# A hybrid decoder layer on one core: sample rows of two norms kept as 128 rows, softmax and value pages at other blocks

## The chip, the cores and the metric

One core of a Trainium2 chip runs the whole layer in one launch. The metric is the device time of the launch in microseconds; the profile below is one execution of the same program.

## The reference, cut to what matters

The layer serves 256 new prompt tokens and 8 sample tokens (one per running sequence), 264 token columns in all, with 2048 channels (16 tiles of 128) and float32 throughout.

```
h  = rmsnorm(x, g1);  proj = h @ w_in               # q k v z xBC dt and two gates
attn = moba_attention(q, k, v)                      # samples: 8 sequences, 8 pages of 128 keys each
ssm  = mamba2(z, xBC, dt)                           # conv, chunked scan, group rmsnorm
m  = sigmoid(ga) * (attn @ w_attn_out) + sigmoid(gs) * (ssm @ w_ssm_out)
x1 = x  + rmsnorm(m @ w_out, g2)                    # second norm
f  = (silu(n @ w_gate) * (n @ w_up)) @ w_down,  n = rmsnorm(x1, g3)
y  = x1 + rmsnorm(f, g4)                            # last norm
rmsnorm(x, g) = x * rsqrt(mean(x*x over the 2048 channels) + 1e-6) * g
```

A sample selects 3 of its 4 past key blocks by score, adds its own key, and takes one softmax over them.

## The kernel before

**Blocks.** The matrix products run over 562 blocks on TensorE. A block is one tile of 128 output channels times eight tiles of input channels: 8 times three products (weights high x input high, high x low, low x high, lines 1733 to 1735), each moving the 264 token columns. Two adjacent output tiles are a pair and share two PSUM banks. Pairs follow a list: the input projection is blocks 0 to 209 (q, dt, k, v, then x, b, c, z and both gates mixed), `so` (w_ssm_out) starts at 210, `ao` (w_attn_out) at 242, `o` (w_out, 8 pairs of 4 blocks) at 258, `gate` and `up` at 290, and `dn` (w_down, 8 pairs of 12 blocks) at 466.

**How a block is fed.** ScalarE rounds the loaded weights to `w_hi` (four slots), VectorE computes `w_lo = raw - w_hi` (line 1197), TensorE waits for it. So ScalarE and VectorE can be at most about three blocks ahead of TensorE.

**Side work.** Every engine walks the same block numbers and issues at fixed numbers whatever else is due: on each engine the order is program order, with semaphores between engines. The numbers that the change touches are written out by hand:

- `K_AT[m] = 30 + int(K_PACE * m)` for the 64 key pages: GpSimd multiplies page m by the query at block K_AT[m] (line 740), VectorE sums it two blocks later (line 1391). With K_PACE 1.58 the last page is at block 129, with 1.61 at block 131.
- `SEL` starts the softmax of the samples. TensorE sums at SEL and SEL+3, VectorE selects at SEL+8 and SEL+9, TensorE turns the maxima at SEL+8 (this needs VectorE's SEL+9), VectorE normalises at SEL+20, and multiplies the own value row (`own_t`) at SEL+24.
- `VG[w]` starts the value pages of samples 2w and 2w+1: eight groups, two blocks apart, on TensorE (line 1985), with VectorE steps at VG+18 and VG+21. The first group waits for `own_t`.
- `UN[g]` are the eight groups of the norm in the state-space branch. VectorE takes the reciprocals at UN[g]+5 (line 1514). The input halves of `so` follow at blocks 211 to 214 (line 1522).

**The last two norms (pairs `o` and `dn`).** After each pair ScalarE leaves the squares of the pair in `sq` and the pair times the gain in `tmp` (128 channels x 264 tokens). `token_sums` on TensorE (from line 2016) turns `tmp` to token rows, per tile: two turns of 128 x 128 (line 1695) into `side[0]` and `side[1]`, and one of 128 x 8 into 8 rows of `side[2]` (line 1696: a plain float32 product with the identity as the moving operand, which appears as two instructions). After every fourth tile VectorE and ScalarE copy 512 columns of the rows out (`rows_of`). After the last pair TensorE sums the squares over channels into `side[3]` (line 2031), three chunks of tokens (128, 128 and 8 rows) times three parts. ScalarE takes the roots (`token_root`), VectorE the reciprocals (`token_rs`).

**Between `o` and `gate`.** `second_norm` on VectorE makes `x1tok = x + norm` in chunks (`x1_chunk`: two of 128 rows and one of 8 rows). TensorE turns it back, tile by tile (`x1_turn`: two turns of 128 x 128 and one of 8 x 128); ScalarE and VectorE make the halves `x_hi`, `x_lo` of the tile (`h_hi_of`, `h_lo_of`). Blocks 290 to 293 are `fresh_products`: per tile k, six products for both output tiles and then the turn of tile k+3. The first three turns lie ahead of the first product, with filler products between them (lines 2049 and 2053). ScalarE squares x1 beside it (`x1_squares`), and the next norm's factor is applied to the outputs of `gate` and `up`.

**The end.** After `dn`, VectorE updates `y` in twelve steps of 512 columns (three token chunks x four), each followed by its store.

Of the kernel before, what the change touches and what calls it, by code (L numbers as in the profile page):

```python
# [22 lines left out]
P = 128  # L23
# [28 lines left out]
K_PACE = 1.58  # L52
# [3 lines left out]
def bass_hybrid_decoder_layer(nc, a, o):  # L56
    ctx = ExitStack()
    with ctx:
# [152 lines left out]
        ftok_s = at("ftok_s", [NB, 2 * 512], fp32, 28 * K)  # L211
        y1s = at("y1s", [NB, D], fp32, E0)
        ftok_e = at("ftok_e", [NB, 2, 512], fp32, E0 + 8 * K)
# [100 lines left out]
        def evac_at(p):  # L314
# [13 lines left out]
        SEL = 130  # L328
        CT_AT = 214
        VG = [152 + 22 * w for w in range(4)]  # L330
        UN = [196, 198, 200, 201, 203, 205, 207, 208]
# [13 lines left out]
            "a_hi_done a_lo_done ao_sum ao_hi ao_lo tk_acc tk_sum tk_tr tk_cp0 tk_cp1 tk_sd m_x1 x1_back x1_out x1_in r2_sd "  # L345
# [9 lines left out]
         tk_tr, tk_cp0, tk_cp1, tk_sd, m_x1, x1_back, x1_out, x1_in, r2_sd, r2_diag, r2_mm, ff_tanh, ff_prod, ff_hi,  # L355
# [73 lines left out]
        y_order = [(0, 0), (0, 1), (1, 0), (1, 1), (0, 2), (1, 2), (2, 2), (2, 0), (2, 1), (3, 2), (3, 0), (3, 1)]  # L429

        def f_part(j, c):

            cols = slice(j * 512, (j + 1) * 512)
            if j == 3:
                return side[c][0:(P if c < 2 else NB), :]
            if c < 2:
                return ftok[:, c, cols]
            return ftok_s[:, cols] if j < 2 else ftok_e[:, 0, :]
# [12 lines left out]
        def _(sp):  # L451
# [157 lines left out]
            def x_again(b):  # L609

                if b == B_O + 8:
                    sp.wait_ge(ao_lo, KT)
                    for c in range(2):
                        sp.dma_start(x1tok[:, c, :], a["x_prompt"][0, c * P:(c + 1) * P, :]).then_inc(x1_back, 16)
                    sp.dma_start(x1tok[0:NB, 2, :], a["x_sample"][:, 0, :]).then_inc(x1_back, 16)
                if b == B_FF + 10:
                    sp.wait_ge(m_x1, 15)
                    for c in range(2):
                        sp.dma_start(x1_spill[c * P:(c + 1) * P, :], x1tok[:, c, :]).then_inc(x1_out, 16)
                    sp.dma_start(x1_spill[TP:T, :], x1tok[0:NB, 2, :]).then_inc(x1_out, 16)  # L620
                if b == B_DN + 8:
# [5 lines left out]
                    sp.dma_start(y1s[:, :], x1_spill[TP:T, :]).then_inc(x1_in, 16)  # L627
# [40 lines left out]
            sp.wait_ge(y_out, 16 * 12)  # L668
# [99 lines left out]
        def _(act):  # L768
# [28 lines left out]
            def h_hi_of(k, gain, m):  # L797

                act.wait_ge(x_tr, KT * m + k + 1)
                func(x_hi[:, k, :], h_bank[m][k % len(h_bank[m])][:, 0:T], scale=gains[:, gain, k:k + 1])\  # L800
# [235 lines left out]
            def rows_of(b, b0, step, base):  # L1036

                j, d = (b - b0) // step - 1, (b - b0) % step
                if 0 <= j < 3 and d == 7:
                    act.wait_ge(tk_tr, base + 4 * j + 4)  # L1040
                    if base:
                        act.wait_ge(mm_done, B_DN)
                        func(ftok[:, 1, j * 512:(j + 1) * 512], side[1][:, :])
                        func(f_part(j, 2), side[2][0:NB, :]).then_inc(tk_cp1, 1)
                    else:
                        cols = slice(j * 512, (j + 1) * 512)
                        func(mtok[:, 1, cols], side[1][:, :])
                        func(mtok[0:NB, 2, cols], side[2][0:NB, :]).then_inc(tk_cp1, 1)

            def token_root(n, summed):  # L1050

                act.wait_ge(tk_sum, summed)
                for c in range(3):
                    rows = P if c < 2 else NB
                    ins = func(nsd[0:rows, n, c:c + 1], side[3][0:rows, 2 * c:2 * c + 1], ACT.Sqrt,
                               bias=eps[0:rows, 0:1], scale=1.0 / D)
                ins.then_inc(tk_sd, 1)

            part = att_st[:, :, :].rearrange("p a b -> p (a b)")

            def x1_squares(j):

                act.wait_ge(m_x1, 3 * j + 6)
                cols = slice(j * 512, (j + 1) * 512)
                for c in range(3):
                    rows = P if c < 2 else NB
                    func(mtok[0:rows, c, cols], x1tok[0:rows, c, cols], ACT.Square,
                         accum_out=part[0:rows, 4 * c + j:4 * c + j + 1])

            def x1_root():  # L1070

                drained(func(mtok[0:1, 0, 0:1], x1tok[0:1, 0, 0:1]))
                for c in range(3):
                    rows = P if c < 2 else NB
                    ins = func(part[0:rows, 4 * c:4 * c + 4], part[0:rows, 4 * c:4 * c + 4],
                               accum_out=nsum[0:rows, 2, c:c + 1])
                drained(ins)
                for c in range(3):
                    rows = P if c < 2 else NB
                    ins = func(nsd[0:rows, 2, c:c + 1], nsum[0:rows, 2, c:c + 1], ACT.Sqrt, bias=eps[0:rows, 0:1],  # L1080
                               scale=1.0 / D)
# [7 lines left out]
            def evac(pr, i, p):  # L1089
# [82 lines left out]
        def _(dve):  # L1172
# [33 lines left out]
            def h_lo_of(k, gain, m):  # L1206

                dve.wait_ge(h_hi, KT * m + k + 1)
                stt(x_lo[:, k, :], h_bank[m][k % len(h_bank[m])][:, 0:T], gains[:, gain, k:k + 1],
                    x_hi[:, k, :].bitcast(fp32), ALU.mult, ALU.subtract).then_inc(h_lo, 1)  # L1210

            def token_rs(n):

                for c in range(3):
                    rows = P if c < 2 else NB
                    ins = v.reciprocal(nrs[0:rows, n, c:c + 1], nsd[0:rows, n, c:c + 1])
                drained(ins)
# [176 lines left out]
            def softmax(b):  # L1394
# [44 lines left out]
                if b == SEL + 24:  # L1439
# [101 lines left out]
            def x1_chunk(j, c0=0, c1=512):  # L1541
# [4 lines left out]
                for c in range(3):  # L1546
                    rows = P if c < 2 else NB
                    m = mtok[0:rows, c, cols] if j < 3 else side[c][0:rows, :]
                    x = x1tok[0:rows, c, cols]
# [562 lines left out]
```

## Time and profile before

| | us |
|---|---|
| median of 3 runs | 1809.43 |
| lowest and highest | 1805.69, 1809.56 |
| the profiled execution's own time | 1807.29 |
| its span in the trace | 1805.5 |
| TensorE busy | 1782.1 (99%) |
| VectorE busy | 1195.2 (66%) |
| ScalarE busy | 918.3 (51%) |
| GpSimd busy | 216.2 (12%) |

Matrix products overlap in the pipeline: a product of 264 columns is shown with 0.28 us, while the next starts 0.12 us later. So what an instruction costs TensorE is read from the starts of its neighbours, not from its duration. A row of the timeline can hold several instructions of one form in a row (x2, x8), with the time from the first start to the last end.

### The profile page before, as it was taken

To read this page: it belongs to the slowest core of one execution; us is meant where nothing else is said; L and a number is where in the kernel's file an instruction comes from. 1 tells how busy PE (TensorE), PEld (TensorE's weight loads), DVE (VectorE), ACT (ScalarE), POOL (GpSimd) and SP (SyncE) were. 2 spreads that over 40 slices of the span, in tenths; PEclk is the share of its full clock that TensorE was granted. 3 is DMA by queue.
4 is the path that set the end of the run, shared out by engine and by line. 5 is a ranking of instruction groups with operands and counts; after the bars stand their busy time and mean duration, and the time that the engine had idled before them with its cause. 6 is when DMAs were issued, how large, how long until landed. Compare 5 with 4: busy or idle time off the path is not lost.

```text
span 1805.5 us, 35392 instructions
## 1 busy us (share of the span) xinstructions
PE 1782.1 (99%) x14613; PEld 1719.1 (95%) x14613; DVE 1195.2 (66%) x1666; ACT 918.3 (51%) x1737; POOL 216.2 (12%) x127
## 2 busy tenths in 40 slices
PE   8999999999999999999999999999999999999997
PEld 8999999998988988889999899999999999999997
DVE  6478999999887557745744666666666666444443
ACT  5544556554766557533444655554545454444342
POOL 2145644564000000000000000000000000000000
PEclk9999999999999999999999999999999999999998
DMA  8589987897789999695564387767777775655552
GB/s 253 177 272 330 320 265 261 278 305 235 222 281 317 303 295 344 217 304 177 180 223 155 116 281 221 225 226 231 230 217 232 229 235 182 216 176 170 175 180 80
DMA packets 397810, 421.40 MB, mean 233 GB/s; under 512 B 13033, under 2 KB 375465, under 8 KB 396585
## 3 DMA queue, kind: packets, MB, share of 16 engines
q10 hardware_dynamic: 284336, 285.35, 49.5%
q1 hardware_dynamic: 112960, 133.11, 22.6%
q8 instruction: 115, 1.88, 0.4%
q0 software_dynamic: 352, 0.67, 0.2%
q14 instruction: 47, 0.38, 0.1%
HBM read 400.70 MB, written 18.66 MB: 232 GB/s over the span
## 4 chain that ended last, share of the span: by engine, by line
PE 87%; DVE 8%; ACT 2%; issue 2%; DMA 0%; ACTq 0%; DVEq 0%; SPq 0%; POOL 0%; POOLq 0%
PE gemm L1733 27%; PE gemm L1734 27%; PE gemm L1735 26%; DVE w_lo L1197 3%; PE side L1985 2%; PE side L1695 1%; DVE conv_out L1189 1%; ACT w_hi L770 1%; DVE sc_flat L1391 1%; PE side L1696 1%; DMA xtok<-in_x_prompt 0%; DVE dec L1186 0%; DVE u L1189 0%; ACT dec L770 0%; PE side L1881 0%
## 5 line engine op out<-in xcount | busy, mean ns | idle before, releaser
L1197 DVE TENSOR_TENSOR w_lo<-raw,w_hi 128x1024 fp32r<-128x1024 f32 (+1 forms) x562 | 737.2, 1315 | 559.2 <-ACT w_hi L770 558.0
L1733 PE MATMUL gemm<-x_hi,w_hi 128*128 128x264 f32 x3312 | 953.1, 288 | 4.9 <-DVE w_lo L1197 3.1
L1735 PE MATMUL gemm<-x_hi,w_lo 128*128 128x264 f32 x3312 | 938.1, 283 | 0.0
L1734 PE MATMUL gemm<-x_lo,w_hi 128*128 128x264 f32 x3312 | 938.0, 283 | 0.0
L770 ACT ACTIVATE w_hi<-raw 128x1024 fp32r<-128x1024 f32 (+1 forms) x562 | 585.9, 1045 | 675.9 <-PE gemm L1735 674.3
L1733 PEld LDWEIGHTS gemm<-x_hi,w_hi 128*128 128x128 f32 x3312 | 623.6, 188 | 34.1 <-issue 25.7
L1734 PEld LDWEIGHTS gemm<-x_lo,w_hi 128*128 128x128 f32 x3312 | 624.4, 189 | 0.9 <-issue 0.5
L1735 PEld LDWEIGHTS gemm<-x_hi,w_lo 128*128 128x128 f32 x3312 | 621.1, 188 | 0.0
L1734 PE MATMUL gemm<-g_lo,w_hi 128*128 128x264 f32 x704 | 200.4, 285 | 0.0
L1733 PE MATMUL gemm<-g_hi,w_hi 128*128 128x264 f32 x704 | 200.1, 284 | 0.0
L740 POOL TENSOR_TENSOR kv<-kv,qb 128x1024 f32<-128x1024 f32 x64 | 177.4, 2780 | 185.1 <-DMA kv<-in_cache_k 185.1
L1735 PE MATMUL gemm<-g_hi,w_lo 128*128 128x264 f32 x704 | 199.6, 283 | 0.0
L1733 PEld LDWEIGHTS gemm<-g_hi,w_hi 128*128 128x128 f32 x704 | 132.6, 188 | 1.5 <-issue 1.5
L1735 PEld LDWEIGHTS gemm<-g_hi,w_lo 128*128 128x128 f32 x704 | 132.6, 188 | 0.0
L1734 PEld LDWEIGHTS gemm<-g_lo,w_hi 128*128 128x128 f32 x704 | 132.2, 188 | 0.0
L1391 DVE TENSOR_REDUCE sc_flat<-kv 128x16 f32<-128x1024 f32 x64 | 77.2, 1206 | 0.0
L1733 PE MATMUL gemm<-m_hi,w_hi 128*128 128x264 f32 x256 | 73.4, 287 | 0.0
L1734 PE MATMUL gemm<-m_lo,w_hi 128*128 128x264 f32 x256 | 72.6, 284 | 0.0
L1735 PE MATMUL gemm<-m_hi,w_lo 128*128 128x264 f32 x256 | 72.5, 283 | 0.0
L770 ACT ACTIVATE stx<-stx 128x128 f32<-128x128 f32 x128 | 37.8, 299 | 29.4 <-DVE stx L1186 29.4
L1733 PEld LDWEIGHTS gemm<-m_hi,w_hi 128*128 128x128 f32 x256 | 48.2, 188 | 1.5 <-issue 1.5
L1734 PEld LDWEIGHTS gemm<-m_lo,w_hi 128*128 128x128 f32 x256 | 48.2, 188 | 0.0
(309 smaller groups left out, 1425.9 us busy)
## 6 DMA issues: line engine op xcount, KB each, us to landing
raw<-in_w_in ACTq DMA_DIRECT2D x99, 1024.0 KB, 7.0
raw<-in_w_gate ACTq DMA_DIRECT2D x44, 1024.0 KB, 5.2
raw<-in_w_up ACTq DMA_DIRECT2D x44, 1024.0 KB, 5.7
raw<-in_w_down ACTq DMA_DIRECT2D x40, 1024.0 KB, 5.3
kv<-in_cache_k SPq DMA_DIRECT2D x64, 512.0 KB, 5.5
kv<-in_cache_v SPq DMA_DIRECT2D x64, 512.0 KB, 5.9
st<-in_state_ssm SPq DMA_DIRECT2D x64, 256.0 KB, 5.3
raw<-in_w_ssm_out ACTq DMA_DIRECT2D x16, 1024.0 KB, 7.2
```

What stands on the lines that cost most here:

```text
L740: gp.tensor_tensor(out=page_slot(m), in0=page_slot(m), in1=qb[:, n % 2, :], op=ALU.mult)\
L770: return nc.scalar.activation(out, in_, f, **kw)
L1189: return v.scalar_tensor_tensor(out=out, in0=x, scalar=scalar, in1=y, op0=op0, op1=op1, **kw)
L1197: v.tensor_tensor(w_lo[:, s, 0:blk.kts, cols], raw[:, s, 0:blk.kts, cols], w_hi[:, b % RING, 0:blk.kts].bitcast(fp32), ALU.subtract).then_ ...
L1391: v.tensor_reduce(out=sc[:, g, n, :], in_=by_head(page_slot(m)), axis=AX.X, op=ALU.add)\
L1695: return nc.tensor.transpose(out, in_, ident[0:k, 0:k])
L1696: return mm(out, in_, ident[0:k, 0:k], start=True, stop=True)
L1733: mm(out, w_hi[:, b % RING, k], pr.hi[:, x], start=(x == 0), stop=False)
L1734: mm(out, w_hi[:, b % RING, k], pr.lo[:, x], start=False, stop=False)
L1735: ins = mm(out, w_lo[:, s, k, cols], pr.hi[:, x], start=False, stop=(x == pr.kt - 1))
L1985: ins = mm(side[3][32 * n:32 * n + 32, :], sc_flat[:, first_col:first_col + 32], page_slot(2 * m + e)[:, half * 512:(half + 1) * 512], sta ...
```

## The change

The eight sample tokens leave the token rows. During `o` and `dn` VectorE copies their columns of `tmp` into `tmps` (128 channels x 8 samples x 16 tiles) after each pair. After the last pair one turn makes 128 rows of it, one for each sample and tile, 128 columns wide. The sum of a sample over its 16 rows comes from a product with a matrix of ones and zeros (`same`, made once from `spread`), or from the summed squares repeated 16 times (`rep`). x1, its spill, the reload and y of the samples have the same form of 128 x 128, so their updates, squares and stores are one each instead of four. The turn back to channels is one, and the sample columns of `x_hi` and `x_lo` are made for all tiles at once. New semaphores order it: `ts_dve`, `ts_pe`, `ts_act`.

```diff
-K_PACE = 1.58
+K_PACE = 1.61
-        SEL = 130
+        SEL = 132
-        VG = [152 + 22 * w for w in range(4)]
-        UN = [196, 198, 200, 201, 203, 205, 207, 208]
+        VG = [154 + 21 * w for w in range(3)] + [218]
+        UN = [196, 198, 199, 201, 202, 204, 205, 206]
...
-                if b == SEL + 24:                       # VectorE: own_t
+                if b == SEL + 23:
-                if b == SEL + 20:                       # TensorE: own factor
+                if b == SEL + 19:
...
# TensorE, token_sums
-                        for c in range(3):
-                            rows = P if c < 2 else NB
-                            ins = mm(side[3][0:rows, 2 * c:2 * c + 2], part[:, c * P:c * P + rows], ones[:, 0:2],
+                        for c in range(2):
+                            ins = mm(side[3][:, 2 * c:2 * c + 2], part[:, c * P:(c + 1) * P], ones[:, 0:2],
...
                     for c in range(2):
-                        turn(side[c][:, cols], tmp[:, n, c * P:(c + 1) * P])
-                    turn(side[2][0:NB, cols], tmp[:, n, TP:T]).then_inc(tk_tr, 1)
+                        ins = turn(side[c][:, cols], tmp[:, n, c * P:(c + 1) * P])
+                    ins.then_inc(tk_tr, 1)
+                if pr.kind == "o" and i == 1:
+                    pe.wait_ge(ts_dve, 1)
+                    mm(side[2][:, 0:P], spread, spread, start=True, stop=True).then_inc(ts_pe, 1)
+                if i == 7:
+                    pe.wait_ge(ts_dve, 6 if base else 2)
+                    pe.wait_ge(ts_act, 1)
+                    rep = mtok[:, 2, 2 * P:3 * P] if pr.kind == "o" else same[:, :]
+                    mm(side[2][:, 128:130], rep, ones[:, 0:2], start=True, stop=True, skip_group_check=True)
+                    turn(side[2][:, 0:P], tmps[:, :, :].rearrange("p b t -> p (b t)")).then_inc(ts_pe, 1)
...
                     for k in range(3):
                         x1_turn(k)
+                        if k == 0:
+                            pe.wait_ge(ts_dve, 3)
+                            turn(side[2][:, 256:384], x1s).then_inc(ts_pe, 1)
# TensorE, x1_turn
                 for c in range(2):
-                    turn(bank[:, c * P:(c + 1) * P], x1tok[:, c, cols])
-                turn(bank[:, TP:T], x1tok[0:NB, 2, cols]).then_inc(x_tr, 1)
+                    ins = turn(bank[:, c * P:(c + 1) * P], x1tok[:, c, cols])
+                ins.then_inc(x_tr, 1)
# TensorE, fresh_products
+                    if x == 0:
+                        pe.wait_ge(ts_dve, 5)
+                    if x == 10:
+                        pe.wait_ge(ts_act, 4)
+                        mm(side[2][:, 130:132], same[:, :], part[:, 8:10], start=True, stop=True).then_inc(ts_pe, 1)
# VectorE, evac of o and dn
+                    sample_columns(i)
...
+                if pr.kind in ("o", "dn") and i == 7:
+                    dve.wait_ge(free_out[par], freed(p))
...
+                    drained(v.tensor_tensor(rep, cols[0], cols[1], ALU.add))
+                    drained(v.tensor_tensor(rep, rep, cols[2], ALU.add))
+                    sample_columns(i).then_inc(ts_dve, 1)
# VectorE, second_norm
                 token_rs(1)
                 x1_chunk(0, 0, P)
+                sample_rs(1, 2)
+                stt(x1s, side[2][:, 0:P], nrs[:, 1, 2:3], x1s, ALU.mult, ALU.add).then_inc(ts_dve, 1)
                 x1_chunk(0, P, 512)
+                dve.wait_ge(ts_pe, 3)
+                mul(hs, side[2][:, 256:384].rearrange("p (b t) -> p t b", t=KT),
+                    gains[:, 2, :].unsqueeze(2).to_broadcast([P, KT, NB])).then_inc(ts_dve, 1)
...
                         h_lo_of(k, 2, 1)
+                        if k == 0:
+                            dve.wait_ge(ts_act, 3)
+                            v.tensor_tensor(x_lo[:, :, TP:T], hs, x_hi[:, :, TP:T].bitcast(fp32), ALU.subtract)\
+                                .then_inc(ts_dve, 1)
# ScalarE, token_root: the two prompt chunks, then
+                act.wait_ge(ts_pe, 2 if n == 1 else 5)
+                func(nsd[:, n, 2:3], side[2][:, 128:129], ACT.Sqrt, ...).then_inc(ts_act, 1)
# ScalarE, after h_hi_of(0)
+                            act.wait_ge(ts_dve, 4)
+                            func(x_hi[:, :, TP:T], hs).then_inc(ts_act, 1)
# ScalarE, rows_of: the copies of 8 rows go; once, at j == 0 of o
+                            act.wait_ge(ts_pe, 1)
+                            func(same[:, :], side[2][:, 0:P]).then_inc(ts_act, 1)
# ScalarE, x1_squares: the four squares of 8 rows go; once
+                    func(mtok[:, 2, 0:P], x1s, ACT.Square, accum_out=part[:, 8:9]).then_inc(ts_act, 1)
# the end
-        y_order = [(0, 0), (0, 1), (1, 0), (1, 1), (0, 2), (1, 2), (2, 2), (2, 0), (2, 1), (3, 2), (3, 0), (3, 1)]
+        y_order = [(0, 0), (0, 1), (1, 0), (1, 1), (2, 0), (2, 1), (3, 2), (3, 0), (3, 1)]
...
-                    sp.dma_start(o["y_sample"][:, 0, cols], y1s[:, cols]).then_inc(y_out, 16)
+                    sp.dma_start(o["y_sample"][:, 0, :].rearrange("b (t p) -> (b t) p", p=P), y1s[:, :]).then_inc(y_out, 16)
```

## Rows read from the trace of the kernel before

**Rows 1.** The page's chain of work that ended last, by engine.

```profile
PE 87%; DVE 8%; ACT 2%; issue 2%; DMA 0%; ACTq 0%; DVEq 0%; SPq 0%; POOL 0%; POOLq 0%
```

**Rows 2.** Stretches: start:end, length, busy by engine, PEclk, DMA share, GB/s.

```profile
377.00:450.00 73.00, 69.92 (x591) 68.10 (x590) 72.83 (x96) 35.09 (x75) 33.43 (x16) 1.00 0.80 252
...
998.00:1005.10 7.10, 6.89 (x50) 5.21 (x50) 3.71 (x12) 2.49 (x8) 0.00 (x0) 1.00 0.00 0
1005.10:1025.20 20.10, 19.55 (x138) 16.75 (x137) 15.46 (x26) 16.65 (x48) 0.00 (x0) 1.00 0.32 105
...
1791.40:1805.50 14.10, 3.12 (x25) 2.14 (x24) 8.29 (x15) 1.30 (x5) 0.00 (x0) 0.65 0.49 154
```

**Rows 3.** Timeline of TensorE, `token_sums` between two blocks: start, length, instruction.

```profile
993.63 0.38 PE L1695 MATMUL side<-ident,tmp 128*128 128x128 f32 x2
993.94 0.39 PE L1696 MATMUL side<-ident,tmp 128*8 128x128 f32 x2
994.25 0.44 PE L1695 MATMUL side<-ident,tmp 128*128 128x128 f32 x2
...
995.16 0.28 PE L1734 MATMUL gemm<-m_lo,w_hi 128*128 128x264 f32 x1
```

**Rows 4.** Timeline of TensorE, the end: sums of two of the three parts.

```profile
1791.76 1.40 PE L2031 MATMUL side<-ones,sq 128*128 128x2 f32 x12
```

**Rows 5.** Timeline of TensorE, eight turns of 128 x 128 between blocks.

```profile
114.97 1.03 PE L1695 MATMUL side<-ident,kT 128*128 128x128 f32 x8
...
115.97 0.29 PE L1734 MATMUL gemm<-x_lo,w_hi 128*128 128x264 f32 x1
```

**Rows 6.** Timeline of TensorE, `x1_turn` inside `fresh_products`.

```profile
1005.83 0.54 PE L1695 MATMUL gemm<-ident,x1tok 128*128 128x128 f32 x3
...
1006.53 0.28 PE L1751 MATMUL gemm<-x_lo,w_hi 128*128 128x264 f32 x1
```

**Rows 7.** Timeline of TensorE, `x_turn` of the first norm: two turns.

```profile
20.67 0.38 PE L1695 MATMUL gemm<-ident,xtok 128*128 128x128 f32 x2
...
21.01 0.28 PE L1734 MATMUL gemm<-x_lo,w_hi 128*128 128x264 f32 x1
```

**Rows 8.** Timeline of VectorE, first steps of `second_norm`.

```profile
1000.62 0.27 DVE L1216 RECIPROCAL nrs<-nsd 128x1 f32<-128x1 f32 x3 [4.42 <-ACT nsd L770]
1000.93 2.45 DVE L1189 SCALAR_TENSOR_TENSOR x1tok<-mtok,nrs,x1tok 128x128 f32<-128x128 f32 x6
```

**Rows 9.** Timeline of VectorE, the end.

```profile
1794.17 2.74 DVE L1189 SCALAR_TENSOR_TENSOR y<-ftok,nrs,y 128x512 f32<-128x512 f32 x4
1796.83 1.39 DVE L1189 SCALAR_TENSOR_TENSOR y1s<-ftok_s,nrs,y1s 8x512 f32<-8x512 f32 x2
```

**Rows 10.** Waits of TensorE: us in total, times, longest.

```profile
PE gemm L1733 <- DVE w_lo L1197: 3.1, 4, 1.7
...
PE gemm L1733 <- DVE x_lo L1522: 1.8, 2, 1.1
PE side L1985 <- DVE own_t L1186: 1.7, 1, 1.7
```

**Rows 11.** Lines 1197 (377:433; 1100:1500) and 1391: count, min/median/max ns, first and last start.

```profile
L1197 DVE TENSOR_TENSOR w_lo<-raw,w_hi x14: 1208/1210/3312, 377.3 to 431.7; 128x1024 fp32r<-128x1024 f32 x14
...
L1197 DVE TENSOR_TENSOR w_lo<-raw,w_hi x138: 1214/1225/1227, 1100.5 to 1498.2; 128x1024 fp32r<-128x1024 f32 x138
...
L1391 DVE TENSOR_REDUCE sc_flat<-kv x64: 1191/1206/1216, 112.5 to 446.3; 128x16 f32<-128x1024 f32 x64
```

**Rows 12.** Timeline of VectorE: end of the selection (SEL+9) and the low half of block 142.

```profile
475.16 2.24 DVE L1419 TENSOR_REDUCE m_w<-sc_flat 128x128 f32<-128x1152 f32 x1
...
483.57 1.22 DVE L1197 TENSOR_TENSOR w_lo<-raw,w_hi 128x1024 fp32r<-128x1024 f32 x1
```

**Rows 13.** Timeline of TensorE: the first product of block 141.

```profile
483.98 0.28 PE L1733 MATMUL gemm<-x_hi,w_hi 128*128 128x264 f32 x1
```

**Rows 14.** Timeline of VectorE: the last reciprocal of UN.

```profile
745.02 1.79 DVE L1514 RECIPROCAL un<-un 128x264 f32<-128x264 f32 x1
```

More of the change, by code:

```diff
@@ L667, in _ @@
             sp.wait_ge(ct_out, 16 * 9)
-            sp.wait_ge(y_out, 16 * 12)
+            sp.wait_ge(y_out, 16 * 9)
             sp.wait_ge(cs_out, 16)
@@ L1057, in token_root @@
                 ins.then_inc(tk_sd, 1)
-            part = att_st[:, :, :].rearrange("p a b -> p (a b)")
+                act.wait_ge(ts_pe, 2 if n == 1 else 5)
+                func(nsd[:, n, 2:3], side[2][:, 128:129], ACT.Sqrt, bias=eps[:, 0:1], scale=1.0 / D).then_inc(ts_act, 1)
             def x1_squares(j):
-                act.wait_ge(m_x1, 3 * j + 6)
+                act.wait_ge(m_x1, 2 * j + 4)
                 cols = slice(j * 512, (j + 1) * 512)
[L1065 to L1068, printed above, removed]
+                for c in range(2):
+                    func(mtok[:, c, cols], x1tok[:, c, cols], ACT.Square, accum_out=part[:, 4 * c + j:4 * c + j + 1])
@@ L1070, in x1_root @@
+                if j == 0:
+                    func(mtok[:, 2, 0:P], x1s, ACT.Square, accum_out=part[:, 8:9]).then_inc(ts_act, 1)
             def x1_root():
                 drained(func(mtok[0:1, 0, 0:1], x1tok[0:1, 0, 0:1]))
[L1073 to L1076, printed above, removed]
+                for c in range(2):
+                    ins = func(part[:, 4 * c:4 * c + 4], part[:, 4 * c:4 * c + 4], accum_out=nsum[:, 2, c:c + 1])
@@ L1077, in x1_root @@
                 drained(ins)
[L1078 to L1081, printed above, removed]
+                func(nsd[:, 2, 0:2], nsum[:, 2, 0:2], ACT.Sqrt, bias=eps[:, 0:1], scale=1.0 / D)
+                act.wait_ge(ts_pe, 4)
+                ins = func(nsd[:, 2, 2:3], side[2][:, 130:131], ACT.Sqrt, bias=eps[:, 0:1], scale=1.0 / D)
@@ L1208, in h_lo_of, with sample_rs @@
                 dve.wait_ge(h_hi, KT * m + k + 1)
-                stt(x_lo[:, k, :], h_bank[m][k % len(h_bank[m])][:, 0:T], gains[:, gain, k:k + 1],
-                    x_hi[:, k, :].bitcast(fp32), ALU.mult, ALU.subtract).then_inc(h_lo, 1)
+                stt(x_lo[:, k, 0:TP], h_bank[m][k % len(h_bank[m])][:, 0:TP], gains[:, gain, k:k + 1],
+                    x_hi[:, k, 0:TP].bitcast(fp32), ALU.mult, ALU.subtract).then_inc(h_lo, 1)
             def token_rs(n):
[L1214 to L1217, printed above, removed]
+                drained(v.reciprocal(nrs[:, n, 0:2], nsd[:, n, 0:2]))
+            def sample_rs(n, rooted=0):
+                wait(dve, ts_act, rooted)
+                drained(v.reciprocal(nrs[:, n, 2:3], nsd[:, n, 2:3]))
             dve.wait_ge(x_in[2], 16)
@@ L1545, in x1_chunk, with sample_columns @@
                     dve.wait_ge(tk_tr, KT)
[L1546 to L1549, printed above, removed]
-                    stt(x, m, nrs[0:rows, 1, c:c + 1], x, ALU.mult, ALU.add).then_inc(m_x1, 1)
+                for c in range(2):
+                    m = mtok[:, c, cols] if j < 3 else side[c][:, :]
+                    x = x1tok[:, c, cols]
+                    stt(x, m, nrs[:, 1, c:c + 1], x, ALU.mult, ALU.add).then_inc(m_x1, 1)
+            def sample_columns(i):
+                return v.tensor_copy(tmps[:, :, 2 * i:2 * i + 2], tmp[:, :, TP:T].rearrange("p n b -> p b n"))
             def second_norm():
```

78 lines of the change are left out of this document (43 added, 35 removed).

## Prediction, made before the changed kernel was run

> **What bounds the kernel now.** I read the chain of waits first [rows 1]: TensorE makes up 87% of it, VectorE 8%. Then the stretches [rows 2]: the granted clock is 1.00 (2.4 GHz) in all of them but the last, where TensorE has stopped. So a microsecond less on TensorE's own queue is a microsecond less of the time, wherever the others keep ahead of it. They fail to do so in few places [rows 10]: four waits for `w_lo`, two for `x_lo`, one for `own_t`. The stretch 377 to 450 is VectorE's: it is busy 72.83 of 73.00 us [rows 2], and two of the `w_lo` waits lie there. From 998.0 to 1025.2 (second norm and the first blocks of `gate`) all three engines hand tiles around, and after 1791.4 VectorE's updates of `y` set the end [rows 2, 9].
>
> **The change part by part.** The sum is made against the profiled execution's 1807.29 us (span 1805.5 and 1.8 around it).
>
> 1. *Turns of `tmp` in `token_sums`, pairs 0 to 6 of `o` and `dn`.* [Rows 3]: from the first turn (993.63) to the second product of the next block (995.16) are 1.53 us. Without side work the block's first product would start where the first turn does, and the second 0.12 later, so turns and switches add 1.41. [Rows 5]: eight turns of 128 x 128, counted in the same way, add 115.97 - 114.97 - 0.12 = 0.88, or 0.11 each. Four turns alone then add 0.44. The two small products, 0.31 us from start to start (993.94 to 994.25), and the switches around them go: 0.97 us per pair. Fourteen pairs of `o` and `dn` have this outside their last: **-13.6 us**. Nothing hides it, for TensorE does not wait there; what is late next is nothing, since ScalarE and VectorE lose work too (the copies of 8 rows; VectorE gains one small copy per pair). Both ends: at least the bare 0.31 per tile, 28 x 0.31 = 8.7; at most 14 x 1.09 = 15.3, if the four turns add no more than 0.08 each.
>
>  By the Trainium skill (TensorE: Matmul & The Clock Gate, section Back-to-back issue gap) a matmul with 128 moving columns starts about 56 ns after the last one. The row disagrees: two such instructions stand 0.31 us in the queue. By the page the 28 small turns would cost 28 x 2 x 0.056 = 3.1 us, and only that would be saved; by the row 13.6. I go by the row.
>
> 2. *Between `o` and `gate`* (7.10 us [rows 2]). TensorE drops the two small turns of the last pair (0.6) and a third of the sums (two parts take 1.40 in [rows 4], three 2.1; a third is 0.7, of which I count 0.5, since the last part waits for ScalarE's `sq` anyway). The rest of the 7.10 is a chain of ScalarE and VectorE: [rows 8] reciprocals 0.27, six updates 2.45, two of the six for samples. These go, but the sample path comes in: two drained sums, one wide update, a reciprocal of its own, the multiplication into `hs`, the copy into `x_hi` on ScalarE and the subtraction into `x_lo`, which the first product waits for (`ts_dve` 5). Queued behind these waits: on TensorE the first block of `gate`, on VectorE `x1_chunk` and all `h_lo_of`, on ScalarE all `h_hi_of`. The filler products on TensorE cover part. Best case -2.5 (the chain shortens as TensorE's part), worst +1.5 (each of five hand-overs adds 0.3 in full, about the step of 0.27 in [rows 8]); I take **-1.3**.
>
> 3. *`fresh_products`.* [Rows 6]: turn to second product with the small turn 0.70 us; [rows 7]: with two turns 0.34. Thirteen turns lie inside: 13 x 0.36 = 4.7. TensorE was busy 19.55 of 20.10 us here [rows 2]; afterwards it needs 15.4, ScalarE's 16.65 loses four squares of 8 rows at about 0.6 to near 14.5, and VectorE's 15.46 loses three updates at 0.68 to near 13.7. The three are then close, so some waits come: 0.7. The product for the samples' sum of squares in tile 10 breaks the stream once: 0.4. Together **-3.6**; bounds -4.7 and -1.5 (ScalarE's 14.5 with the handing over of today's 20.10 - 16.65 = 3.45 left in full gives 18.0, or -2.1).
>
> 4. *The end.* [Rows 9]: an update takes 2.74/4 = 0.68 us, and one with 8 rows as much (1.39/2). Four of these go; one of 128 columns (2.45/6 = 0.41, the mean of the narrower ones in [rows 8]) and a reciprocal of its own (0.27 at most) come: -2.0. Ahead of them 0.5 goes for the sums, as in part 2, and 0.5 for one root and two reciprocals (estimated from the 0.27 for three). **-3.0**; the nine stores instead of twelve keep pace behind. The sample's store has 128 rows of 512 bytes instead of 8 rows of 2 KB; two stores follow it, so it hides unless it lands more than one update later (+0.7, the worst end of this part).
>
> 5. *First value group.* It stood 1.7 us behind `own_t` [rows 10]. TensorE reaches it at 154, VectorE makes `own_t` at 155: one block ahead instead of two. A block is 2.9 us or more, so the wait goes: **-1.7**; what is late next (the factor at SEL+19 on TensorE against VectorE's SEL+20) has about 1.5 us to spare. Value groups one block closer per pair leave the page loads four blocks, and their landing is hidden.
>
> 6. *UN two blocks earlier.* Two waits for `x_lo`, 1.8 us in total, longest 1.1 [rows 10]. The reciprocals (1.79 us each, [rows 14]) leave blocks 212 and 213 of VectorE and come to 210 and 211. The later wait goes. The earlier one stays in my reckoning, for the last reciprocal now lies right ahead of the first `x_lo`. The new order makes ScalarE wait for TensorE's group 5 ahead of group 7; it has two blocks in hand. **-1.2**; bounds -1.8 and +1.0.
>
> 7. *K_PACE.* In 377 to 433 VectorE is never idle, so TensorE's waits there are VectorE's surplus of work. Up to block 126 one page sum less is due (60 instead of 61, from the formula): 1.21 us [rows 11]. One GpSimd multiplication less falls in as well. [Rows 11]: the same `w_lo` takes 1.21 at least and up to 3.31 while GpSimd multiplies keys, and 1.22 to 1.23 with GpSimd idle, so collisions cost up to 2.1 each. The Trainium skill (GPSIMD Engine Reference, section Specifications) says that GpSimd's memory interfaces are shared with VectorE when VectorE's instruction has two inputs from SBUF; the trace agrees with 3.31 against 1.21. The new pace reshuffles the collisions: **-1.5**, bounds -4 and +3.
>
> 8. *Softmax two blocks later.* The selection (4.0 us, its last step in [rows 12]) moves behind VectorE's conv work of block 141, and TensorE waits for it after block 140. Work that VectorE has finished at 483.57 [rows 12] is the same in either order, and TensorE comes to that point at 483.98 [rows 13]; but in the new order VectorE idles earlier, up to 1.7 us, for ScalarE's halves. Wait 0 to 2: **+1.0**.
>
> 9. *New products* (`spread`, once; switches around it): **+0.5**.
>
> Sum: -13.6 -1.3 -3.6 -3.0 -1.7 -1.2 -1.5 +1.0 +0.5 = **-24.4 us**. Against its own time that is 1782.9; against the median 1809.43, which lies 2.1 above the profiled execution, 1785.0. I take 1784.
>
> **Rivals.**
> - *The middle turns worse* (places 7 and 8): collisions in the VectorE-bound stretch and the selection each at their bad end, +3 and +2 for -1.5 and +1, the UN order at +1.0: 7.7 above the forecast, about 1792. For it: VectorE has 0.2 us left in 73 [rows 2]. Against it: every moved piece is moved later or into slack.
> - *The middle turns better*: all waits of [rows 10] go (3.1 + 1.8 + 1.7 = 6.6, where I count 4.4) and the end of the stretches is at its best: 1778.
> - *A small turn costs no more than its moving columns*, 0.11 us as a turn of 128 x 128 does [rows 5], and the rest of the gaps in [rows 3] stays with the remaining turns: part 1 falls to 28 x 0.11 = 3.1, the time is 1794.5. For it: the wide turns behind a small one are further apart than in [rows 5] too. Against it: eight of them in a row need 0.11 each.
>  This is the case in which the page on TensorE would be right.
> - *The clock falls* in the stretch after 998, if the sample path leaves TensorE idle where it is busy 6.89 of 7.10 us now [rows 2]. At 1.2 GHz the 15.4 us of part 3 would take 31: about 1800. Against it: the fillers stay, and the clock was 1.00 there.
> - *Slower than before*: the key multiplications fall on `w_lo` halves all the way from 377 to 450. Place: TensorE waits on line 1733; price up to 2.1 each [rows 11]. Sixteen GpSimd instructions lie there [rows 2]: up to 33.6 us, where the sum without part 7 saves 22.9, so 1818. It decides from the eleventh further full collision on. Against it: the order of both engines changes by at most two blocks, and the present trace has only a handful.
>
> **How the numbers follow.** Forecast 0.66, the middle worse 0.13, the middle better 0.12, small turns cheap 0.04, clock 0.03, slower 0.02. The range 1777 to 1792 holds the first three and leaves the rest. A measurement of this kernel can't tell 0.2% (3.6 us) from nothing; faster by more than that takes 0.97, within it 0.01, slower 0.02.
>
> **What would show it.** Part 1: between two blocks of `o` or `dn` four turns, and the second product 0.56 us after the first turn instead of 1.53. Part 2: the first product of `gate` less than 6.5 us after the sums start. Part 3: block 294 starts within 17 us after that, instead of 20.1. Part 4: nine updates, the end within 12 us of the last product. Parts 5 and 6: no wait for `own_t`, at most one for `x_lo`. Parts 7 and 8: waits for `w_lo` between 377 and 450 below 2 us, and a new wait of TensorE at the turn of the maxima after block 140. I am wrong if the turns alone still take over 0.8 us per pair, or if the middle loses more than 5 us.

## The result, and the profile after

| | before | after |
|---|---|---|
| median | 1809.49 (4 runs, 1805.69 to 1810.13) | 1792.20 (4 runs, 1789.74 to 1793.96) |
| the profiled execution's own time | 1807.29 | 1789.74 |
| its span | 1805.5 | 1788.2 |

The ratio is 0.9906, 95% interval [0.9894, 0.9917]: 17.3 us faster, where 24.4 were forecast. 1792.2 lies 8.2 us above the forecast of 1784 and 0.2 us outside the range given, on the side of the rival "the middle turns worse". The direction was right, the sum 7 us too large.

**The turns (part 1).** The timeline of TensorE after, between two blocks of `o`: start, length, instruction. It answers [rows 3].

```profile
991.03 0.60 PE L1725 MATMUL side<-ident,tmp 128*128 128x128 f32 x4
991.39 0.37 PE L1763 MATMUL gemm<-m_hi,w_hi 128*128 128x264 f32 x1
991.60 0.28 PE L1764 MATMUL gemm<-m_lo,w_hi 128*128 128x264 f32 x1
```

Four turns in a row, and the second product 0.57 us after the first turn, where it was 1.53 and 0.56 was forecast.

**The stretches.** Stretches of the trace after, columns as in [rows 2]: the one that VectorE bounds, from the sums to the first product of `gate`, `fresh_products`, and from the last sums to the end.

```profile
377.00:450.00 73.00, 69.47 (x592) 68.13 (x591) 72.83 (x95) 33.83 (x67) 32.25 (x17) 1.00 0.81 259
994.38:999.94 5.56, 5.00 (x43) 4.53 (x41) 3.89 (x13) 2.71 (x9) 0.00 (x0) 1.00 0.00 0
999.94:1017.01 17.07, 16.15 (x126) 15.04 (x125) 14.03 (x26) 14.85 (x43) 0.00 (x0) 1.00 0.39 124
1775.91:1788.20 12.29, 2.37 (x21) 2.09 (x19) 6.73 (x14) 1.44 (x5) 0.00 (x0) 0.62 0.56 177
```

7.10 us became 5.56, and 20.10 became 17.07. But in the first row VectorE is as full as it was (72.83 of 73.00), and TensorE does a little less than before (69.47 for 69.92).

**The waits.** TensorE's waits after: us in total, times, longest. They answer [rows 10].

```profile
PE gemm L1763 <- DVE w_lo L1198: 3.5, 4, 2.0
PE side L1725 <- DVE x_lo L1190: 2.0, 1, 2.0
PE gemm L1763 <- DVE x_lo L1525: 1.9, 2, 1.2
...
PE side L1989 <- issue: 1.4, 1, 1.4
PE side L1725 <- DVE m_w L1422: 1.1, 1, 1.1
...
PE side L2005 <- DVE m_w L1434: 0.5, 1, 0.5
```

`own_t` is gone. The waits for `w_lo` (3.1 before) and for the `x_lo` of `so` (line 1525, 1.8 before) are no shorter than they were, and three are new: 1.4 for the products over the page sums (line 1989, at SEL; put down to "issue", but they follow the last page sum on VectorE, two blocks later in this schedule: it ends at 456.76, they start at 456.87), and 1.1 and 0.5 for the softmax (`m_w`). The wait of 2.0 in the second row ends at 17.6 us, in the first norm (0.6 in the first trace of before, 1.8 in a second one), and block 113 still starts when it did.

**Where the time went.** The start of the first product of each block, less its start in the first trace of before, both counted from ScalarE's first `w_hi`. I worked these out from the timelines; the last two columns belong to kernels described below.

| first product of block | after | after, second trace | before, second trace | rows alone | rows and value groups |
|---|---|---|---|---|---|
| 113 | 0.0 | 0.0 | 0.0 | 0.0 | 0.0 |
| 126 | 0.5 | 5.0 | 0.4 | -0.2 | -0.3 |
| 133 | 1.7 | 6.7 | 0.4 | 1.0 | 1.0 |
| 152 | 3.9 | 10.5 | 0.4 | 1.1 | 1.0 |
| 154 | 1.3 | 7.8 | 2.4 | 3.0 | -1.5 |
| 197 | 2.6 | 9.2 | 2.4 | 3.0 | -0.1 |
| 258 (middle done) | 2.7 | 9.2 | 2.4 | 3.0 | -0.1 |
| 289 (`o` nearly done) | -3.6 | 3.0 | 2.4 | -3.3 | -6.4 |
| 290 (first of `gate`) | -5.2 | 1.4 | 2.4 | -4.9 | -8.0 |
| 298 | -8.4 | -1.9 | 2.4 | -8.1 | -11.3 |
| 561 (last of `dn`) | -15.3 | -8.8 | 2.4 | -15.0 | -18.1 |

Each entry is from one execution. Column "after": the middle, where I had forecast -3.4 (parts 5 to 8), lost 2.7. Everything behind it follows the forecast closely. The second traces say more: two executions of the same kernel differ in the middle by 2.4 us (before) and 6.5 us (after).

### The profile page after: what moved, and what is told of

It is laid out like the page before. It is cut to its first block, busy times and chain, and to the rows that moved or that the text cites. A ratio compares the mean times of both kernels' runs of the same rounds, so it can differ in the third digit from the quotient of the medians.

```text
span 1788.2 us, 35230 instructions
## 1 busy us (share of the span) xinstructions
PE 1761.8 (99%) x14532; PEld 1712.6 (96%) x14532; DVE 1201.9 (67%) x1679; ACT 912.9 (51%) x1724; POOL 214.4 (12%) x127
## 4 chain that ended last, share of the span: by engine, by line
PE 90%; DVE 7%; ACT 1%; issue 1%; DMA 0%; DVEq 0%; ACTq 0%; SPq 0%
PE gemm L1763 28%; PE gemm L1764 28%; PE gemm L1765 28%; DVE w_lo L1198 3%; PE side L2020 2%; PE side L1725 1%; DVE conv_out L1190 1%; ACT w_hi L772 1%; DVE sc_flat L1394 1%; DMA xtok<-in_x_prompt 0%; DVE un L1517 0%; DVE u L1190 0%; PE side L1916 0%; DVE dec L1187 0%; PE side L1898 0%
```

## The experiments

Medians of the kernels before, of the same chips, were 1809.7 to 1810.0.

**Experiment 1: the sample rows alone.** The changed kernel with the old numbers.

```diff
-K_PACE = 1.61
+K_PACE = 1.58
...
-        SEL = 132
+        SEL = 130
...
-        VG = [154 + 21 * w for w in range(3)] + [218]
-        UN = [196, 198, 199, 201, 202, 204, 205, 206]
+        VG = [152 + 22 * w for w in range(4)]
+        UN = [196, 198, 200, 201, 203, 205, 207, 208]
```

(own_t at SEL+24 and its factor at SEL+20 again.)

> The changed kernel with every constant of before (K_PACE 1.58, SEL 130, VG and UN of before, own_t at SEL+24, its factor on TensorE at SEL+20): the sample rows' part alone. Theory A (the rows' part gives what its stages show, about 20 us, and the rescheduled middle costs 2.7): 20 us below before, 1789.5, and 2 to 3 us below the full change. Theory B (the middle was sized rightly at -3.4, and the sample rows' part gives only 14, what I read as the middle's loss being a shift of the trace): 1795.5, slower than the full change by 3.

Measured: 1789.31 (1786.47 to 1790.16), ratio 0.9881 [0.9866, 0.9895], or -20.7 us against 1809.97. Theory A said -20, and parts 1 to 4 and 9 of the prediction add up to -21.0. Theory B falls.

**Experiment 2: the new order alone.** The kernel before with the new numbers.

```diff
-K_PACE = 1.58
+K_PACE = 1.61
...
-        SEL = 130
+        SEL = 132
...
-        VG = [152 + 22 * w for w in range(4)]
-        UN = [196, 198, 200, 201, 203, 205, 207, 208]
+        VG = [154 + 21 * w for w in range(3)] + [218]
+        UN = [196, 198, 199, 201, 202, 204, 205, 206]
...
-                if b == SEL + 24:
+                if b == SEL + 23:
...
-                if b == SEL + 20:
+                if b == SEL + 19:
```

> The kernel before with the new constants alone (K_PACE 1.61, SEL 132, VG [154, 175, 196, 218], the new UN, own_t at SEL+23, its factor on TensorE at SEL+19). Theory A: +2.7 us, so about 1812, with new waits of TensorE at the products of the page sums (block 133) and at the turn of the maxima (after block 140), and none for own_t. Theory B: -3.4 us, 1806.

Measured: 1812.18 (12 runs), ratio 1.0014 [1.0005, 1.0024]: slower by 2.2 us, where the prediction's parts 5 to 8 have -3.4. Its waits, in the stretch 440 to 530, are the forecast ones of theory A:

```profile
PE side L1954 <- issue: 1.5, 1, 1.5
PE side L1695 <- DVE m_w L1419: 1.1, 1, 1.1
PE side L1970 <- DVE m_w L1431: 0.5, 1, 0.5
```

So the order of work, not the sample rows, holds most of the miss: 5.6 of the 7 us.

**Experiments 3 and 4: which of the numbers.** The full change with the old pace, and the full change with the old UN.

```diff
-K_PACE = 1.61
+K_PACE = 1.58
```

> The changed kernel with K_PACE 1.58 and the rest of the new constants kept (softmax at SEL 132, new VG, new UN). Theory A1 (the later page sums are what makes TensorE wait at block 133, 2.1 us, and the collisions at blocks 110 to 114): 2 us faster than the full change, 1790, with block 133 starting without a wait. Theory A2 (the pace is innocent, the selection moved behind the conv work of block 141 costs it): the same as the full change within 0.5 us.

Measured: 1788.03 (1786.09 to 1789.33), ratio 0.9882 [0.9867, 0.9896]. The full change, taken again on another chip, was 1792.26 (1788.63 to 1796.21), ratio 0.9899 [0.9884, 0.9914]. All eight runs of the full change have a median of 1792.3, so the pace costs 4.2 us; the intervals of the ratios overlap a little, and 4.2 is good to about 2. The traces agree in direction: from the start of block 113 to that of block 133 the four traces with pace 1.61 take 3.3 us more than the first of before on average (0.5, 1.7, 4.1 and 6.7), the seven with 1.58 take 0.4 more (-2.5 to 2.5). In the trace with the old pace TensorE doesn't wait at block 133: the last page sum ends at 445.47, ahead of block 131. Theory A1 stands.

```diff
-        UN = [196, 198, 199, 201, 202, 204, 205, 206]
+        UN = [196, 198, 200, 201, 203, 205, 207, 208]
```

> The changed kernel with the UN list of before ([196, 198, 200, 201, 203, 205, 207, 208]). By my reading of the trace after, the new list gives nothing (one of the two waits for x_lo goes, the other stands one block earlier and longer): within 0.5 us of the full change. By my forecast (-1.2 for the new list) this kernel would be 1.2 us slower than the full change.

Measured: 1790.25 (1787.43 to 1794.83). That is 2 us less than the full change, within the scatter of both, where the forecast wants 1.2 more. The trace tells it better than the median: from block 197 to 213, where UN acts, the full change loses 0.1 us (2.61 to 2.69) and this kernel nothing (2.96 to 2.95), both against before. So the new UN gave nothing in these traces.

**Experiment 5: the value groups alone, and the best kernel.** The full change with K_PACE, SEL and UN of before (own_t at SEL+24 again); only VG stays new, so the first value group stands at block 154 with `own_t` made at 154.

> The changed kernel with K_PACE 1.58, SEL 130 and the old UN, but the new VG ([154, 175, 196, 218]): the sample rows and the later value groups alone, without the later softmax. Theory A (the wait for own_t, 1.7 us, is the only thing that the later order removes, and the value group at 154 alone removes it): 1.7 below the rows alone, about 1787.6, no wait for own_t and none for the selection. Rival (the wait is only exchanged for one further on, at the next page sums or softmax steps): 1789.3 as with the rows alone.

Measured: **1786.79** (1785.39 to 1787.58), ratio 0.9873 [0.9858, 0.9888]. It has the lowest median of the kernels that compute everything: 5.4 us below the full change, and 2.5 below the rows alone (this last difference lies within the intervals). Its trace has neither the wait for `own_t` nor the three new ones.

**Experiment 6: both kernels once more.** Before and after, unchanged.

> The kernel before itself, unchanged, to see how far two profiled executions of one kernel lie apart in the stretch that VectorE bounds (blocks 113 to 150). Theory A (key multiplications of GpSimd meet other w_lo halves in each execution): TensorE's waits for w_lo between 370 and 640 differ by 1 to 3 us from the first trace, and the rest agrees within 0.2 us. Theory R (the order of work fixes the collisions): the waits agree within 0.3 us.

> The full change again, beside the others on one chip. If its first trace (2.7 us lost in the middle) was typical: again 1792 and again 2 to 3 us behind a kernel with the rows alone (1789.5). If it was a bad draw of the collisions: 1790 or less.

Measured: before 1810.59 (1807.41 to 1813.36), after 1792.26, so the full change comes out at 1792 again. For before neither theory fits: the waits for `w_lo` between 370 and 640 are 2.0 us in the second trace and 2.5 in the first, block 152 starts only 0.4 us later, and then 2.0 more are lost behind the same wait for `own_t` (1.8 us, 1.7 in the first trace). The thing that no theory had is easiest to see in the trace of the rows alone, behind that wait. Its timeline:

```profile
527.43 1.06 PE L2020 MATMUL side<-kv,sc_flat 128*32 128x512 f32 x8 [1.79 <-DVE own_t L1187]
528.43 0.39 PE L1763 MATMUL gemm<-x_hi,w_hi 128*128 128x264 f32 x1
528.65 0.29 PE L1764 MATMUL gemm<-x_lo,w_hi 128*128 128x264 f32 x1
528.78 0.29 PE L1765 MATMUL gemm<-x_hi,w_lo 128*128 128x264 f32 x1
528.90 0.33 PE L1763 MATMUL gemm<-x_hi,w_hi 128*128 128x264 f32 x1
529.03 0.42 PE L1764 MATMUL gemm<-x_lo,w_hi 128*128 128x264 f32 x1
529.25 0.42 PE L1765 MATMUL gemm<-x_hi,w_lo 128*128 128x264 f32 x1
529.47 0.42 PE L1763 MATMUL gemm<-x_hi,w_hi 128*128 128x264 f32 x1
```

Shortly behind the wait the products stand 0.22 us apart instead of 0.12. The stretches of the same trace (columns as in [rows 2]), and of the first trace of before around its own wait of 1.7 us:

```profile
524.00:527.40 3.40, 1.42 (x11) 0.94 (x9) 3.38 (x8) 1.59 (x9) 2.07 (x1) 1.00 1.12 345
527.40:532.50 5.10, 5.07 (x29) 4.23 (x29) 2.26 (x2) 3.75 (x10) 1.19 (x2) 0.67 1.07 378
532.50:540.00 7.50, 7.50 (x62) 6.52 (x61) 4.38 (x9) 6.94 (x21) 0.00 (x0) 1.00 1.09 355
```

```profile
527.00:532.00 5.00, 5.00 (x43) 4.76 (x40) 2.29 (x3) 4.04 (x10) 0.46 (x1) 1.00 1.07 369
```

A granted clock of 0.67 over 5.1 us: TensorE ran at 1.2 GHz for about three microseconds, 15 products each 0.10 late and one 0.05, 1.6 us in all. In before's first trace the clock stayed at 2.4 GHz behind the same wait. So the wait for `own_t` costs 1.7 us in one execution and 3.4 (1.8 and 1.6) in another, and removing it can be worth more than its length. The same happened behind long waits for `w_lo`. In the second trace of the full change TensorE waits 3.62 us and then runs slowly (start, length, instruction, wait ahead; below it the stretch 414 to 420):

```profile
416.16 0.59 PE L1763 MATMUL gemm<-x_hi,w_hi 128*128 128x264 f32 x1 [3.62 <-DVE w_lo L1198]
416.55 0.42 PE L1764 MATMUL gemm<-x_lo,w_hi 128*128 128x264 f32 x1
416.77 0.42 PE L1765 MATMUL gemm<-x_hi,w_lo 128*128 128x264 f32 x1
```

```profile
414.00:420.00 6.00, 3.84 (x17) 3.84 (x18) 5.93 (x8) 0.00 (x0) 3.54 (x2) 0.58 0.35 101
```

23 products at 0.22 us cost 2.3 us on top of the 3.6. This execution lost 9.2 us in the middle, where the first lost 2.7.

**Experiment 7: no collisions.** Two kernels in which GpSimd multiplies only the first 64 of 1024 columns of each page: the full change, and the best kernel. The other 960 columns stay unmultiplied, so their scores aren't those of the layer; loads, waits and VectorE's sums stay.

```diff
-gp.tensor_tensor(out=page_slot(m), in0=page_slot(m), in1=qb[:, n % 2, :], op=ALU.mult)
+gp.tensor_tensor(out=page_slot(m)[:, 0:64], in0=page_slot(m)[:, 0:64], in1=qb[:, n % 2, 0:64], op=ALU.mult)
```

> The full change, but GpSimd's key multiplication covers only the first 64 of the 1024 columns of each page (the other columns of the keys stay unmultiplied, so the scores differ; all waits, loads and VectorE's sums stay). Theory C (GpSimd's multiplications stretch VectorE's instructions, and this is the main part of what the middle loses and of its scatter): at least 3 us faster than the full change (1792.2), 1789 or less, no w_lo above 1.4 us between 377 and 450, no stretch with the clock below 1.00 there. Theory O (the new order's own work is late, collisions or not): the wait at the products of the page sums stays above 1 us and the time within 1.5 us of 1792.

> The kernel with sample rows and later value groups alone, with the same short key multiplications (64 of 1024 columns). Beside the full change with short keys it tells what the new pace, the later softmax and the new UN cost when there are no collisions. Theory C: what is left is the wait of TensorE for the selection (1.1 and 0.5), so 1 to 2 us between the two. Theory O: 4 us or more between them, as with full multiplications.

Measured: 1784.30 (1783.86 to 1785.65), 8.0 us below the full change, and 1782.60 (1782.20 to 1784.64), 4.2 below the best kernel. Between the two are 1.7 us, theory C's 1 to 2, where the same two kernels with full multiplications are 5.4 apart: about 3.7 of what the new pace, softmax and UN cost come only with the multiplications. VectorE's low halves between 372 and 436, busy us and mean ns of one: the full change in its first and its second trace, the best kernel, and the full change with short keys.

```profile
L1198 DVE TENSOR_TENSOR w_lo<-raw,w_hi 128x1024 fp32r<-128x1024 f32 x18 | 31.9, 1782 | 0.0
```

```profile
L1198 DVE TENSOR_TENSOR w_lo<-raw,w_hi 128x1024 fp32r<-128x1024 f32 x15 | 30.7, 2060 | 0.0
```

```profile
L1198 DVE TENSOR_TENSOR w_lo<-raw,w_hi 128x1024 fp32r<-128x1024 f32 x18 | 28.7, 1605 | 2.7 <-ACT w_hi L772 2.7
```

```profile
L1198 DVE TENSOR_TENSOR w_lo<-raw,w_hi 128x1024 fp32r<-128x1024 f32 x20 | 24.3, 1220 | 7.6 <-ACT w_hi L772 7.6
```

The same instruction takes 1.78 and 2.06 us on average in these two traces with the new pace, 1.61 in the one with the old, and 1.22 without the multiplications. Over all traces the averages are 1.66 to 2.11 in the four with pace 1.61 and 1.45 to 1.72 in the seven with 1.58. Without the multiplications VectorE even waits 7.6 us for ScalarE, no `w_lo` wait is left between 377 and 640, and only the two waits for `m_w` (1.1 and 0.5) stay, which are the 1.7 between the two kernels. I also summed, over all of VectorE's instructions that start between 372 and 436, what each takes above the shortest of its form in the trace: 12.9 to 14.9 us in the seven traces with pace 1.58, 13.7, 15.0, 16.8 and 20.1 in the four with 1.61, and 1.0 and 1.2 in the two with short multiplications. So it is the multiplications that leave VectorE short in the middle. The new pace adds about 2 us of this on average, but one execution with it (13.7) lies among those with the old.

The multiplications fall at other places in each execution: counted from the first `w_hi`, those of the two traces of before start up to 6.3 us apart, those of the full change up to 5.2. What moves them is in the row on who GpSimd waits for ahead of its multiplications (line 742 of the full change: us, times):

```profile
L742 POOL TENSOR_TENSOR kv<-kv,qb x64: 2382/2454/3800, 101.9 to 440.9; 128x1024 f32<-128x1024 f32 x64
...
  DMA kv<-in_cache_k: 192.4, 44
```

44 of 64 multiplications start when their page lands, not when the program order lets them. The Trainium skill (SBUF — State Buffer, section Who interferes with whom) says that a VectorE instruction with two inputs from SBUF, as `w_lo` is, contends with a GpSimd instruction that reads SBUF, and that the port pair which they share is an exclusive lock. The trace agrees: the longest `w_lo` is 3.43 us, 2.2 over its 1.21, and a multiplication takes 2.4 at least.

**Experiment 8: a faster pace.** The best kernel with K_PACE 1.52.

> Sample rows and later value groups alone, with K_PACE 1.52 in place of 1.58: the last page sum lies at block 127 instead of 131, so about three page sums more (1.21 us each) are done ahead of the stretch in which VectorE is short of time. If VectorE's surplus of work in 113 to 130 is what TensorE waits for there: waits for w_lo 1 to 2 us less, 1785.5. Rival (the sums only move the shortage to earlier blocks, where GpSimd and the page loads are then late): 1787 to 1790.

Measured: 1788.05 (1785.51 to 1791.59). Not faster, as far as four runs that spread over 6 us can tell: the waits for `w_lo` are 2.0 us in its trace (of the fastest run) for 3.9 in the best kernel's. The pace of 1.58 stays as good as any I tried. By the time its rival held; by which mechanism isn't shown.

**Experiment 9: the small turns together.** The kernel before, both turns of 8 columns behind all four wide ones.

```diff
                     for c in range(2):
                         turn(side[c][:, cols], tmp[:, n, c * P:(c + 1) * P])
+                for n in range(2):
+                    t = 2 * i + n
+                    cols = slice(t % 4 * P, t % 4 * P + P)
                     turn(side[2][0:NB, cols], tmp[:, n, TP:T]).then_inc(tk_tr, 1)
```

> The kernel before with the two small turns (8 sample rows) of each pair of o and dn put behind the four turns of 128 x 128 instead of one behind every two: the same instructions, one switch between wide and small turns fewer. Theory S (a good part of the 0.97 us per pair is the switch between outputs of 128 and of 8 partitions): 0.15 to 0.3 us less per pair, 16 pairs, so 2.5 to 5 us faster, 1805 to 1807. Theory O (each small turn has a cost of its own, 0.31 us from start to start, wherever it stands): no change, 1810 within 1.

Measured: 1805.05 (11 runs), ratio 0.9979 [0.9970, 0.9988], 4.8 us faster with the same instructions. The timeline of TensorE, one pair of `o`:

```profile
996.34 0.60 PE L1695 MATMUL side<-ident,tmp 128*128 128x128 f32 x4
996.87 0.60 PE L1696 MATMUL side<-ident,tmp 128*8 128x128 f32 x4
997.40 0.39 PE L1733 MATMUL gemm<-m_hi,w_hi 128*128 128x264 f32 x1
997.63 0.29 PE L1734 MATMUL gemm<-m_lo,w_hi 128*128 128x264 f32 x1
```

From block to block a pair takes 1.43 us before, 1.19 here, and 0.48 after the change (starts of the products around them). Theory S holds: of the 0.95 us that the change saves per pair, 0.24 is one change from wide to small turns and back, and 0.71 the small turns with the other such change; of these, 0.53 pass from the first small turn to the next product (996.87 to 997.40).

**Experiment 10: the sample store last.** The best kernel with another order of the last updates.

```diff
-        y_order = [(0, 0), (0, 1), (1, 0), (1, 1), (2, 0), (2, 1), (3, 2), (3, 0), (3, 1)]
+        y_order = [(0, 0), (0, 1), (1, 0), (1, 1), (2, 0), (2, 1), (3, 0), (3, 1), (3, 2)]
```

> Sample rows and later value groups alone, with the sample's update and store after those of the last column group (the small store last, the two stores of 256 KB one step earlier). Theory T (the end is set by the stores that queue up behind one another, and the small one with rows of 512 bytes takes less after the big ones): 0.5 to 1 us faster, 1786. Rival (the small store's landing, last of all, is what then ends the kernel, or its update waits): same or up to 0.7 slower.

Measured: 1787.75 (1785.66 to 1789.08) for 1786.79: the rival. From the sums to the end the traces have 12.7 us here and in the best kernel; the last update ends 4.4 and 4.5 us ahead of the end. The 1.0 between the medians isn't in the end: this kernel's trace has a `w_lo` wait of 3.2 us in the middle, with the clock down behind it.

## Why the prediction was right and where it was wrong

- **Part 1** (-13.6): right. -6.3 over the pairs of `o` and -6.9 over those of `dn`, 13.1 in all. The -6.3 hold **part 9** (+0.5) too: the block with the new product is 0.6 us longer than its like behind the other pairs (3.85 for 3.26), so part 1 alone is -13.7. The row was the better guide than the Trainium skill's figure (TensorE: Matmul & The Clock Gate, Back-to-back issue gap), by which 3.1 would have been saved. That section gives the 56 ns for a product by itself and about 81 ns where each product loads its weights, as here; by that the estimate is 56 instructions times 0.081, or 4.5, and the row still disagrees. Experiment 9 shows what the row held: a small turn and, apart from it, the change to small turns and back.
- **Part 2** (-1.3): -1.6. **Part 3** (-3.6): -3.0 up to block 294, which comes 17.07 us after block 290 (I had put "within 17"), and -3.3 up to 298.
- **Part 4** (-3.0): mis-sized, -2.0. VectorE's timeline of the end, answering [rows 9]:

```profile
1778.32 4.07 DVE L1190 SCALAR_TENSOR_TENSOR y<-ftok,nrs,y 128x512 f32<-128x512 f32 x6
1782.49 0.35 DVE L1190 SCALAR_TENSOR_TENSOR y1s<-side,nrs,y1s 128x128 f32<-128x128 f32 x1
1782.76 1.40 DVE L1190 SCALAR_TENSOR_TENSOR y<-side,nrs,y 128x512 f32<-128x512 f32 x2
```

 The updates take 5.84 us (1778.32 to 1784.16) for 8.02 before, -2.2 as reckoned. Ahead of them 0.6 went instead of 1.0 (2.41 for 2.97 from the first sum, 1791.20 before, to the first update). Behind them 0.7 came: 4.04 us from the last update to the end for 3.31. I wrote that "the nine stores instead of twelve keep pace behind". They don't quite. Before, the samples' four stores of 16 KB lay between stores of 256 KB, and the DMA rate fell to 6 GB/s beside them; after the change it stays at 205 GB/s or more until the last store is nearly out. That this backlog is what costs the 0.7 is my reading, and no run tests it.
- **Part 5** (-1.7): the wait went as forecast. Its price was too small for the executions in which the clock fell behind it: by the medians of experiments 1 and 5 its going gave 2.5, though their intervals overlap.
- **Part 6** (-1.2): wrong, 0.1 lost. "The later wait goes": it did (1.05 us, ending at 751.26), but the earlier one grew from 0.72 to 1.25 and another of 0.65 came behind it (ending at 748.05): 1.9 us in two waits for 1.8 in two.
- **Part 7** (-1.5): the step that failed, +4.2 by the medians of experiment 3 and +2.9 by the traces up to block 133. I counted one page sum (1.21) less due by block 126 as gain and took the collisions as reshuffled evenly. With the later pace VectorE lost about 2 us more to collisions, on average and not in every execution (experiment 7), and the last sum went behind more of VectorE's work: it ends at 456.76, where it ended at 447.48, and TensorE waits for it (1.4 to 1.9 us), where it came 1.4 us after it before. I had given this the bound +3.
- **Part 8** (+1.0): the two waits for `m_w`, 1.6 us, and 1.7 by experiment 7. Right in kind, within the bounds 0 to 2.
- **Rivals.** "The middle turns worse" is what came: 1792, and I gave it 0.13. It had the right places (7, 8 and the UN order), and its argument against, that "every moved piece is moved later or into slack", was the wrong one: later was into the stretch without slack. That the time came so near its 1792 is partly luck, for the end was mis-sized by 1.0 as well, and single runs of the full change go from 1788.6 to 1796.2. The clock did fall in some executions, but not where I looked for it: behind 998 it stayed at 1.00.
- **Signs.** Three more of those that I named failed: the waits for `w_lo` between 377 and 450 are 2.8 us ("below 2"), there are two waits for the `x_lo` of `so` ("at most one"), and the end takes 12.3 us from the last product ("within 12"). The middle lost 2.7 us in one execution and 9.2 in the other, and "more than 5" was my sign of being wrong.

The miss in the terms of the runs: rows alone -20.7, value groups -2.5, softmax two blocks later with the new UN +1.2 (1788.03 less 1786.79), pace +4.2. These are the steps of one chain from before to the full change, so that they add up to its gain is no check of them, and each is good to 1 to 2 us. The forecast had -21.0, -1.7, -0.2 and -1.5 for the same steps.

What stays open: how often the clock falls behind a wait of 1.7 to 2 us. Among these traces it did behind three waits for `own_t` (1.8 each), behind or in four for `w_lo` (3.6, 3.6, 3.2 and 2.0) and behind one of 1.9 at line 1989, and not behind a `w_lo` wait of 2.0 (the full change), one of 1.8 at line 1989 (old UN) and the 1.7 for `own_t` of before's first trace. What decides it isn't shown. Filling the wait with other products wasn't tried.

## What to carry to other kernels

Take a change in pieces when it has pieces: the rows were worth 20.7 us and one constant beside them took 3 to 4 back, and a median of the whole couldn't tell. Where one engine is full, ask of a later due time what it lands on, and read the mean length of an instruction of fixed shape over that stretch, for it shows collisions that no wait is named for. And price a wait of TensorE above its length, because the clock may fall behind it.

## What the runs showed of the hardware

- A low half of 128x1024 on VectorE takes 1.22 us with GpSimd quiet and up to 3.43 beside GpSimd's multiplications of 128x1024 (2.4 us each). They cost the best kernel 4.2 us and the full change 8.0. The scatter is smaller without them too: 1.8 and 2.4 us between the slowest and fastest of four runs, for 2.2 to 7.6 in the eight other series of runs with the sample rows.
- Behind a wait of TensorE of 1.8 us its clock was 0.67 over the next 5.1 us (1.6 us lost), in one execution; behind the like wait of 1.7 us in the first trace of before it stayed at 1.00. The slow level is 1.2 GHz, the other 2.4: the products stand 0.22 and 0.12 us apart.
- Turns with an output of 8 partitions, one behind the other, instead of between wide ones: 0.24 us less per pair of tiles, with the same instructions (1.19 for 1.43).
